# Router logits from raw rows, normalisation folded in afterwards, and the block table built after the one-hots

## The reference

```python
h = layer_norm(alpha * h + gate * mixer_out, ln_g, ln_b)      # shortened
t = h * (1 + scale2) + shift2
scores = jax.nn.sigmoid((t @ w_router).astype(jnp.float32))
sel = scores + router_bias.astype(jnp.float32)
...
_, eidx = lax.top_k(jnp.where(emask, sel, -jnp.inf), TOP_K)
wts = jnp.take_along_axis(scores, eidx, 1)
...
hid = jax.nn.silu(xblk @ w_gate[e]) * (xblk @ w_up[e])
return hid @ w_down[e]
```

## Time and profile before

| | us |
|---|---|
| median of 3 runs | 1338.87 |
| lowest and highest | 1338.63, 1342.88 |
| the profiled execution's own time | 1337.26 |
| its span in the profile | 1335.5 |
| PE busy | 1089.7 (82%) |
| DVE busy | 498.2 (37%) |
| ACT busy | 222.0 (17%) |
| POOL busy | 255.6 (19%) |

### The profile page before, as it was taken

One profiled execution on the slowest core, in us unless ns is written; L12 is line 12 of the kernel. 1 busy time (PEld: TensorE's weight loads), 2 busy tenths in 40 slices (PEclk: granted clock), 3 DMA queues, 4 the chain that ended last, 5 costly groups with the idle time before them and its releaser, 6 DMA issues.

```text
span 1335.5 us, 27302 instructions
## 1 busy us (share of the span) xinstructions
PE 1089.7 (82%) x10504; PEld 636.4 (48%) x10505; DVE 498.2 (37%) x1237; ACT 222.0 (17%) x680; POOL 255.6 (19%) x309
## 2 busy tenths in 40 slices
PE   4999799997993999998985199989938999988950
PEld 1444344444452566665653144444525666665630
DVE  0246544354456223222222511224572232232227
ACT  0222333333110111111101210120101111111110
POOL 0002100000001223323221250500012332232323
PEclk9999899999995999999988599999859999999985
DMA  8921299992342794899994774133429869999943
GB/s 324 383 104 63 102 353 354 363 349 96 140 165 76 251 383 144 324 376 374 383 382 158 254 270 175 64 115 137 158 75 329 312 213 314 381 383 378 383 168 126
DMA packets 149928, 329.84 MB, mean 247 GB/s; under 512 B 10905, under 2 KB 23617, under 8 KB 149761
## 3 DMA queue, kind: packets, MB, share of 16 engines
q1 hardware_dynamic: 122400, 286.88, 59.3%
q10 hardware_dynamic: 21056, 22.78, 5.1%
q0 software_dynamic: 6432, 19.67, 4.4%
HBM read 312.51 MB, written 25.17 MB: 253 GB/s over the span
## 4 chain that ended last, share of the span: by engine, by line
PE 68%; DVE 11%; SPq 6%; DMA 5%; issue 5%; ACT 4%; ACTq 0%; POOL 0%; DVEq 0%; POOLq 0%
PE PS L1330 18%; PE PS L1346 10%; PE PS L1268 8%; PE PS L1394 8%; PE PS L1178 7%; SPq L318 4%; PE PS L1198 3%; PE PS L1114 3%; PE PS L1209 2%; DMA RD<-expert_rows,yidx 2%; DVE RE L1033 2%; DMA ring<-in_e_down_dram 2%; DVE mx L814 2%; DMA ring<-in_w_ada_dram 1%; ACT RE L664 1%
## 5 line engine op out<-in xcount | busy, mean ns | idle before, releaser
L1330 PE MATMUL PS<-ring,RE 128*32 128x256 f32 x3520 | 205.9, 386 | 22.7 <-issue 14.7
L1330 PEld LDWEIGHTS PS<-ring,RE 128*32 128x32 f32 x3520 | 133.5, 112 | 87.9 <-issue 36.7
L1033 DVE TENSOR_TENSOR RE<-RE,PS 64x128 f32<-64x128 f32 x160 | 39.7, 288 | 258.1 <-ACT RE L664 258.1
L1346 PE MATMUL PS<-ring,RE 128*32 128x256 f32 x1760 | 108.1, 386 | 11.7 <-ACT RE L667 10.7
L664 ACT ACTIVATE RE<-PS 64x128 f32<-64x128 f32 x160 | 34.5, 264 | 489.9 <-PE PS L1330 485.0
L1268 PE MATMUL PS<-ring,uT 128*128 128x512 f32 x256 | 111.2, 593 | 1.9 <-ACT G L628 1.1
L1394 PE MATMUL PS<-ring,uT 128*128 128x512 f32 x256 | 110.0, 592 | 0.0
L1330 PE MATMUL PS<-uT,RE 128*32 128x256 f32 x768 | 89.2, 384 | 7.4 <-issue 5.2
L1039 DVE TENSOR_TENSOR RE<-PS,G 128x256 f32<-128x256 f32 x80 | 34.0, 425 | 155.3 <-PE PS L1346 155.3
L1330 PE MATMUL PS<-RD,RE 128*32 128x256 f32 x768 | 88.8, 385 | 0.0
L1178 PE MATMUL PS<-ring,uT 128*128 128x512 f32 x192 | 84.4, 592 | 0.0
(11 more groups left out here) (231 smaller groups left out, 1348.3 us busy)
## 6 DMA issues: line engine op xcount, KB each, us to landing
ring<-in_w_ada_dram SPq DMA_DIRECT2D x24, 2048.0 KB
ring<-in_e_gate_dram SPq DMA_DIRECT2D x22, 2048.0 KB
ring<-in_e_up_dram SPq DMA_DIRECT2D x22, 2048.0 KB
ring<-in_e_down_dram SPq DMA_DIRECT2D x22, 2048.0 KB
RD<-in_e_up_dram SPq DMA_DIRECT2D x10, 2048.0 KB
RFW<-in_e_down_dram SPq DMA_DIRECT2D x10, 2048.0 KB
uT<-in_e_gate_dram SPq DMA_DIRECT2D x10, 2048.0 KB
expert_rows<-RE ACTq DMA_DIRECT2D x320, 32.0 KB
```

Of the source, the lines that this page charges most:

```text
L1033: V_.tensor_tensor(hid[:, P * h:P * h + P], gs[:, P * h:P * h + P], PS[2 * BLK:P, 0, P * h:P * h + P], ALU.mult).then_inc(hid_rd[l][h], 1)
L1330: ins = mm(PS[BLK * q:BLK * q + BLK, 0, 0:256], xT[:, k, :], w[:, k, 256 * h:256 * h + 256], start=(k == 0), stop=(k == DC - 1))
L1346: ins = mm(PS[BLK * q:BLK * q + BLK, 5, 0:256], hidT[:, h, k // 2, :], wd[:, k, 256 * q:256 * q + 256], start=(k == 0), stop=(k == FC - 1))
```

## The change

**Raw rows are turned.** `turn_tile` no longer waits for the normalised tile. It takes `H` as summed (new semaphore `h_add`) and stands between the two halves of the next tile's product. ACT alone copies both halves, as two 512-wide `ACT.Copy` (L659), without scale and shift, and takes the square root of the tile after them. ACT also normalises the tile for the store (`norm_and_store`, L652); for the last tile it does so after the sigmoid. DVE no longer normalises or copies turned tiles.

**The norm is folded in.** With h a raw row, rs its inverse deviation and nb = -mean*rs, the logits are rs*(h . w*fsc) + nb*(sum of w*fsc) + (sum of w*fsh). DVE scales the router weights once per layer into `wrf` (L898). PE takes the two sums over the depth with eight matmuls of 2 stationary and 16 moving columns (L1334), and spreads them over the partitions (L1338); DVE builds the offset of each tile (`offset`, L909) and the logits at the end (L951).

**Four column groups.** `route_parts` (L1307) runs eight matmuls whose stationary side is 32 columns of folded router weights and whose moving side is 128 token columns; four go to four column groups of the array. The four partial sums lie in four partition groups. DVE copies them out (`parts_copy`, L905), and one matmul (`route_sum`, L1316) turns and adds them.

**The table moves.** The block count of an expert comes from two 16-wide operations in place of a 240-wide comparison and reduction (L1003, L1004). The two slot products and reductions become one pair, twice as wide (L1029, L1030). The block table and order list are made behind the one-hots, and POOL waits for them after the first gathers. The spreading of the second gate's columns (`gate_cols` in `moe`) moves ahead of the product as `g2c`.

Per-layer semaphores are merged into running ones; the core of the diff:

```diff
-                pool.wait_ge(tab_rd, l + 1)
...
+                pool.wait_ge(tab_rd, l + 1)
...
+                def norm_and_store(j):
+                    act.wait_ge(h_ab, NT * l + j + 1)
+                    A(H[:, j, :], H[:, j, :], ACT.Identity, bias=nb[:, j:j + 1], scale=rs[:, j:j + 1]).then_inc(h_nrm, 1)
+                    act.wait_ge(h_nrm, NT * l + j + 1)
+                    act.dma_start(hscr[l][j * P:(j + 1) * P, :], H[:, j, :]).then_inc(s_hw[j], 16)
+
                 for j in range(NT):
...
+                    for half in range(2):
+                        act.wait_ge(h_pe, 2 * NT * l + 2 * j + half + 1)
+                        A(uT[:, 4 * half:4 * half + 4, j * P:(j + 1) * P], PS[:, 4 + half, :].rearrange("p (f s) -> p f s", f=4),
+                          ACT.Copy).then_inc(h_act, 1)
+                    act.wait_ge(hv_rd, NT * l + j + 1)
+                    A(rt[:, j:j + 1], ms[:, j:j + 1], ACT.Sqrt).then_inc(hs_rd, 1)
+                    if j < NT - 1:
+                        norm_and_store(j)
+                A(warm[:, :], ones[:, 0:1], ACT.Sigmoid)
+                act.wait_ge(lc_rd, l + 1)
+                A(sc_[:, :, :], sel[:, :, :], ACT.Sigmoid).then_inc(sig_rd, 1)
+                norm_and_store(NT - 1)
...
+                V_.tensor_tensor(wrf[:, :, 0:NE], wr[:, :, :], fsc[:, 2 * l, :].unsqueeze(2).broadcast_to([P, DC, NE]),
+                                 ALU.mult).then_inc(fw_rd, 1)
+
+                def parts_copy(j):
+                    dve.wait_ge(rt_pe, NT * l + j + 1)
+                    if j:
+                        dve.wait_ge(lg_pe, NT * l + j)
+                    V_.tensor_copy(lgT, PS[:, 6, 0:P]).then_inc(lt_rd, 1)
+
+                def offset(j):
+                    dve.wait_ge(h_ab, NT * l + j + 1)
+                    return V_.scalar_tensor_tensor(out=lofs[:, j, :], in0=lcol[:, 1, :], scalar=nb[:, j:j + 1],
+                                                   in1=lcol[:, 0, :], op0=ALU.mult, op1=ALU.add)
+
                 for j in range(NT):
+                    if j >= 2:
+                        affine(l, j - 2)
                     for n in range(2):
...
-                        link(V_.scalar_tensor_tensor(out=h, in0=h, scalar=ALPHA if l == 0 else 1.0, in1=r,
-                                                     op0=ALU.mult, op1=ALU.add))
+                        V_.scalar_tensor_tensor(out=h, in0=h, scalar=ALPHA if l == 0 else 1.0, in1=r,
+                                                op0=ALU.mult, op1=ALU.add).then_inc(h_add, 1)
+                        dve.wait_ge(h_add, 2 * (NT * l + j) + n + 1)
                         ins = V_.bn_stats(st6[:, j, 6 * n:6 * n + 6], h)
-                    ins.then_inc(mx_used[l], 1)
...
+                    if j == 0:
+                        dve.wait_ge(fr_pe, l + 1)
...
+                    if 0 < j < NT - 1:
+                        parts_copy(j - 1)
+                    rsqrt(1, hs_rd, NT * l + j + 1, j)
+                    if j == NT - 1:
+                        parts_copy(j - 1)
+                    V_.scalar_tensor_tensor(out=nb[:, j:j + 1], in0=mv[:, j, 0:1], scalar=-1.0, in1=rs[:, j:j + 1],
+                                            op0=ALU.mult, op1=ALU.mult).then_inc(h_ab, 1)
+                    if j == 1:
+                        dve.wait_ge(fl_pe, l + 1)
+                        V_.tensor_copy(lcol, PS[:, 7, 192:224].rearrange("p (v e) -> p v e", v=2)).then_inc(fr_rd, 1)
+                        dve.wait_ge(fr_rd, 2 * l + 2)
+                        offset(0)
                     if j:
-                        tile_turned(l, j - 1)
-                    rsqrt(1, hs_rd[l], j + 1, j)
-                    norm_tile(H, j, h_nrm[l])
-                    if 0 < j < NT - 1:
-                        affine(l, j - 1)
-                tile_turned(l, NT - 1)
+                        ins = offset(j)
+                parts_copy(NT - 1)
+                link(ins)
+
+                def logits(j):
+                    dve.wait_ge(lg_pe, NT * l + NT)
+                    return V_.scalar_tensor_tensor(out=sel[:, j, :], in0=PS[:, 7, NE * j:NE * j + NE], scalar=rs[:, j:j + 1],
+                                                   in1=lofs[:, j, :], op0=ALU.mult, op1=ALU.add)
+
+                for j in range(NT):
+                    ins = logits(j)
+                ins.then_inc(lc_rd, 1)
...
+                link(V_.tensor_scalar(nbk[:, :], PS[:, 5, 64:80], 1.0, float(BLK) / 2 - 0.5, ALU.max, ALU.add))
+                link(V_.tensor_scalar(nbk[:, :], nbk[:, :], 1.0 / BLK, float(1 << 23), ALU.mult, ALU.add))
+                V_.tensor_scalar(nbk[:, :], nbk[:, :], float(1 << 23), None, ALU.subtract)
...
+                link(V_.tensor_tensor(both, smap[:, :, :].unsqueeze(1).broadcast_to([P, 2, NT, NE]), o12[:, :, :, :], ALU.mult))
+                link(V_.tensor_reduce(slot[:, :, :], both, AX.X, ALU.add))
...
             def turn_tile(l, j):
 
-                pe.wait_ge(h_nrm[l], j + 1)
+                n = NT * l + j
+                for half in range(2):
+                    pe.wait_ge(h_add, 2 * n + half + 1)
+                    if j:
+                        pe.wait_ge(h_act, 2 * n + half - 1)
+                    for f in range(4):
+                        at = 512 * half + P * f
+                        ins = nc.tensor.transpose(PS[:, 4 + half, f * P:(f + 1) * P], H[:, j, at:at + P], ident[:, :])
+                    ins.then_inc(h_pe, 1)
+
+            def route_parts(l, j):
+
+                n = NT * l + j
+                pe.wait_ge(h_act, 2 * n + 2)
                 if j:
...
+                    pe.wait_ge(lt_rd, n)
+                for kk in range(2):
+                    for g in range(4):
+                        ins = mm(PS[32 * g:32 * g + 32, 6, 0:P], wrf[:, 2 * g + kk, :], uT[:, 2 * g + kk, j * P:(j + 1) * P],
+                                 start=(kk == 0), stop=(kk == 1))
+                ins.then_inc(rt_pe, 1)
+
+            def route_sum(l, j):
+
+                if j == 0:
+                    pe.wait_ge(fr_rd, 2 * l + 2)
+                pe.wait_ge(lt_rd, NT * l + j + 1)
+                mm(PS[:, 7, NE * j:NE * j + NE], lgT, sum4[:, :], start=True, stop=True).then_inc(lg_pe, 1)
 
             def project(l, n):
 
                 w = weights(n), weights(n + 1)
                 for j in range(NT):
                     if j >= 2:
-                        pe.wait_ge(mx_used[l], j - 1)
+                        pe.wait_ge(mx_used, NT * l + j - 1)
                     for half in range(2):
                         for k in range(DC):
                             ins = mm(PS[:, 2 * (j % 2) + half, :], uT[:, k, j * P:(j + 1) * P], w[half][:, k, :],
                                      start=(k == 0), stop=(k == DC - 1))
                         ins.then_inc(y_pe[l], 1)
-                    if j >= 1:
-                        turn_tile(l, j - 1)
+                        if j and half == 0:
+                            turn_tile(l, j - 1)
+                    if j == 0:
+                        pe.wait_ge(fw_rd, l + 1)
+                        for k in range(DC):
+                            ins = mm(PS[0:2, 7, 128:144], fold2[:, k, :], wr[:, k, :], start=(k == 0), stop=(k == DC - 1))
+                        ins.then_inc(fr_pe, 1)
+                    if j == 1:
+                        pe.wait_ge(fr_rd, 2 * l + 1)
+                        mm(PS[:, 7, 192:224], ones[0:2, :], frow.rearrange("p v e -> p (v e)"), start=True, stop=True
+                           ).then_inc(fl_pe, 1)
+                    if j:
+                        route_parts(l, j - 1)
                     if j >= 2:
-                        route_tile(l, j - 2)
-                route_tile(l, NT - 2)
+                        route_sum(l, j - 2)
                 turn_tile(l, NT - 1)
-                route_tile(l, NT - 1)
+                route_sum(l, NT - 2)
+                route_parts(l, NT - 1)
+                route_sum(l, NT - 1)
```

More of the change, by code:

```diff
@@ L151, in backbone @@
         cand = sb("cand", [P, NT, NE])
-        o1 = sb("o1", [P, NT, NE])
-        o2 = sb("o2", [P, NT, NE])
+        o12 = sb("o12", [P, 2, NT, NE])
+        o1, o2 = o12[:, 0, :, :], o12[:, 1, :, :]
+        both = RW[:, 2736:2736 + 2 * NT * NE].rearrange("p (k t e) -> p k t e", k=2, t=NT)
         MP = sb("MP", [P, NT + 1, NE])
@@ L229, in backbone @@
         s_zero, s_fold = sem("pads_zeroed"), sem("folded_ready")
-        mx_used = [sem(f"mixer_tile_used_{l}") for l in range(DEPTH)]
-        hv_rd = [sem(f"tile_var_ready_{l}") for l in range(DEPTH)]
-        hs_rd = [sem(f"tile_std_ready_{l}") for l in range(DEPTH)]
-        h_nrm = [sem(f"tile_normed_{l}") for l in range(DEPTH)]
-        h_pe = [sem(f"tile_turned_in_psum_{l}") for l in range(DEPTH)]
-        h_act = [sem(f"tile_turned_by_act_{l}") for l in range(DEPTH)]
-        h_dve = [sem(f"tile_turned_by_dve_{l}") for l in range(DEPTH)]
+        mx_used = sem("mixer_tile_used")
+        hv_rd = sem("tile_var_ready")
```

(30 more changed lines are left out.)

114 lines of the change are left out of this document (42 added, 72 removed).

## The result

| | before | after |
|---|---|---|
| median of the runs, us | 1339.55 (runs beside it) | 1330.1 (1328.18 to 1332.92, 4 runs) |
| ratio, 95% interval | | 0.9927, 0.991 to 0.9945 |
| span of the profiled execution, us | 1335.5 | 1331.1 |
| product start to first block, layer 0 | 99.41 | 93.86 |
| product start to first block, layer 1 | 100.44 | 92.63 |

A forecast was written before the change was run, and what follows sets the result against it. PE held 68% of the path, and from product end to first block everything was one thread. Layer 0's -6.4 and layer 1's -8.4 us made -14.8: 1337.3 to 1322.5, plus 1.6 for the median, 1324.1 us; range 1319.5 to 1330.5.

The forecast's parts named there:

- a late DVE: Rival in the product: DVE's chain fits or misses by 0.3 us; if late, about 1328 us; chance 0.13.
- a lost gain of layer 0: Rival: expert weight loads set layer 0's loop end, only layer 1's 8.4 us stay, 1330.5 us; chance 0.05.
- The product, before E: Term for w_o's output product: 3.44 us removed, 4.8 added, so its end comes 1.4 us later; bounds 0.9 to 3.0.
- E: The moment the last w_o matmul of a layer's mixer output product ends; 391.13 us in layer 0 before.
- the rule weighed there: Changing tiling mode drains TensorE, four more entries a layer; at another 0.2 us each the time would be 1325.7.
- The low prices: Lower bounds of the product's added costs: it ends 0.9 us later; all terms low, the total gain is 17.9 us.
- E to the sigmoid: Term from product end to router sigmoid: E + 7.2 us, saving 5.3 in layer 0 and 7.3 in layer 1.
- Nearly the same figure in each layer: Sign of being right: the sigmoid starts 6.3 to 7.6 us after E, nearly alike in both layers.
- Sigmoid to index: Term from sigmoid to the cast gather index: 18.3 us in place of 20.8, net 2.5 saved in each layer.
- The groups run together: Negates a rival on router logits: four column groups not running together, 1333.5 us, chance 0.04.
- The first block 6 us and 15 us earlier: Sign of being right: the first gathered block comes 6 us earlier in layer 0 and 15 us in layer 1.
- the profiled execution, 1337.3, becomes 1322.5: Summing step: the whole 14.8 us gain comes off the profiled execution; the run median stands 1.6 above it.

The follow-up runs named there:

- The third profile: The changed kernel run again without edits, its third trace: median 1326.97 us, ratio 0.9909; profiled execution 1324.56 us, without the clock fall in attention.
- its second profile: The kernel before, run again without edits for a second trace: 1339.15 us, ratio 0.9998.
- attention held: Fifteen unread matmuls keep TensorE busy in attention's thin end: 1324.0 us in the changed kernel, 1336.96 us in the kernel before.
- the same filler: The fifteen unread matmuls in attention's thin end, added to the changed kernel (ratio 0.9873) and to the kernel before (ratio 0.9967).
- the routing filler: Changed kernel with unread matmuls at five places between the product and the first block of each layer: 1320.89 us; with attention's extra matmuls too, 1319.77 us.

## Why the forecast held, and where it was off

The forecast was a gain of 14.8 us and 1324.1 us. The median came at 1330.1, inside the range by 0.4 us. That it lies inside is luck: the upper end was there for a late DVE or for a lost gain of layer 0, neither of which came. The terms that the change itself sets were right to about half a microsecond each.

- **The product, before E: forecast +1.4, measured +1.9** (60.62 us for 58.75 from start to last matmul). The terms were near: sets of partial logits were priced 0.5 and cost 0.57, sum and spreading 0.33 each for 0.5 together, the eight fold matmuls 0.48 for 0.7. They make 1.45. What no term had is the half product behind the fold matmuls and behind a set, 7.06 for 6.87 each time, 0.38 in all. That is what the rule weighed there predicts, 0.2 for each visit, found here at 0.19. The Trainium skill (TensorEngine Tiling (Array Packing), Key Properties) says that a change of tiling mode drains TensorE, and the trace agrees with it, at that price. The 6.96 behind a sum is not part of it: in the kernel before, a tile behind the plain router product took 13.84 for 13.74 too.
- **Its bounds do not follow from its prices.** The low prices give 1.1 and not 0.9, the high ones 2.7 and not 3.0. Summed with the other bounds the gain runs from about 10.5 to 17.4 us, where 9.5 to 17.9 stands. The forecast does not hang on this, and the range goes wider than either.
- **E to the sigmoid: forecast E + 7.2, measured E + 7.48 and 7.47.** "Nearly the same figure in each layer" was right here; in the two other profiles of the changed kernel it was 7.47 and 7.68, and 7.46 and 7.67. The clock fell at E + 4.5 in both layers (before, in layer 1, at E + 3.3), so that the first sum escaped it. The small DVE steps were as priced (copies 0.30 for 0.29), but four logits took 0.68 for 0.5. At full clock it was 6.82 for 6.3.
- **Sigmoid to index: forecast 18.3, measured 18.39** in both layers.
- **DVE late: did not happen.** DVE sat idle for 0.24 us before tile 3's last half in both layers and met E within 0.03; the estimate "it fits or misses by 0.3" was close.
- **The groups run together:** 0.57 a set. The gathers waited for the index and not for the stored rows.
- **Layer 0's gain lost in the weight loads: did not happen in the changed kernel.** The third profile starts the loop 6.3 us earlier than before (425.50 for 431.79) and takes 290.8 us for 293.4. But the ground given for it, a DMA share of 0.37 between 500 and 530, looked at the wrong place: at the end of that loop, from 665 to 715, PE waits 6.0 us for weights in the kernel before already (4.9 in its second profile), and 4.5 to 4.8 in the three profiles of the changed one.
- **"The first block 6 us and 15 us earlier": failed in both layers of the first profile** (431.13 for 431.79, with the fall at 320.5, and 989.71 for 998.92). In the profile without the fall it came 6.3 us earlier in layer 0 and 16.3 in layer 1.

The step that failed is "the profiled execution, 1337.3, becomes 1322.5". It took the one profile's attention as fixed. That profile belonged to the group without the fall, while the median of the changed kernel lies near executions with it: its profiled runs were 1332.92 and 1330.87 with, 1324.56 without. Of the miss of 6 us, 1.4 are the terms (13.4 for 14.8), 0.7 the base (the runs of before beside it have 1339.55, the runs shown 1338.87), and the rest, about 4, is laid to the fall. That 4 is a remainder and not a measurement, but it is the size by which the product started late, 3.9 us without the microsecond lost before it. Compared with attention held in both, the change gives 1336.96 - 1324.0 = 13.0 us (across two chips), 4.6 of it from routing and 8.4 from the router logits; profile against profile without the fall it is 1335.5 - 1322.7 = 12.8. That the held kernel came out at 1324.0 where 1324.1 was forecast is partly luck, since the base gains 3.4 us by the same filler.

Three things stay open. Of the nine profiles five of the seven that have the change or a part of it show the fall, and none of the two of the kernel before; the filler gained about 6 us in the one (3.0 to 7.1 by the median that it is compared with) and 3.4 in the other. Whether the change makes a late attention more likely, or these were chance, nine are too few to say, and no run tried what sets its start. The tail behind the last block took 48.8 to 49.8 us in the changed kernel's three profiles for 47.7 and 48.8 before, but 47.8 with attention held. And layer 1's loop was longer in those three. No run here looked into either.

## What to carry to other kernels

Before a gain is read off two profiles, split both spans at landmarks that the edit does not touch; a stretch of foreign code that moved by microseconds (here 4.9) is another effect, and it can hide half of an edit (2.1 for 4.6). Where PE works in short bursts with gaps, hold its clock with matmuls that nothing reads: here fifteen of them were worth about 6 us to the changed kernel (1324.0 for 1330.2, the median of its 15 runs on three chips; 3.0 against the best of the three) and 3.4 to the kernel before. A fix in one place may meet the next bound at once: the routing filler brought 9 us alone and 4 beside the other.

## What was not expected of the hardware

- Whether TensorE's clock fell in a given stretch went with where the stretch lay in time: in nine profiles the same instructions with the same gaps ran at 1.00 when attention's first value group began at or before 183.96 us, and the clock fell to 0.50 some 136 to 137 us later when it began at 184.18 or after. Whether the start is the cause no run shows.
- At the first gathered block the clock was still at half for most of 64 matmuls (to 436.5 of 437.4 in after), 6.31 us for 3.66. No view of waits shows that, since PE is busy there. From first to second block the kernel before took 8.34 and 8.38 us in layer 0 and the changed one 9.50, 8.18 and 8.25; in layer 1 it was 8.83 and 9.18 for 9.14, 9.77 and 10.28, so a part of layer 1's gain went back there.
- A set of partial logits in four column groups cost 0.57 us at full clock and 1.05 at half, and 0.19 more in the product behind it. Its copies and sums at the end made the sigmoid later than the plain form did (E + 7.48 for E + 6.11), though it won in all by the shorter product.
